# The end of the dilated-attention stage: output weights and seven of eight result rows split during the last segment, and most of the output projection issued ahead of the last merges

## The reference

```python
def dilated_attention_mixer(h, w_in, w_out, rel_bias):
    proj = h @ w_in                       # q, k, v of three groups, and the gate z
    for g, (window, dilation) in enumerate(DILATED_GROUPS):
        o, l = dilated_group_attention(q[g], k[g], v[g], rel_bias, window, dilation)
    wts = jax.nn.softmax(jnp.stack(lses), axis=0)
    o = jnp.sum(wts[..., None] * jnp.stack(outs), axis=0)
    return (o * jax.nn.silu(z)) @ w_out   # the "result" times the output weights
...
h = rms_norm(x, attn_pre_norm)
h = dilated_attention_mixer(h, attn_w_in, attn_w_out, rel_bias)
x = x + rms_norm(h, attn_post_norm)
```

## Time and profile before

| what | us |
|---|---|
| median of 3 runs | 3506.31 (3500.53 to 3507.26) |
| profiled execution, its own time | 3508.67 |
| its span | 3506.3 |
| TensorE matmul busy in the span | 3275.6 (93%) |
| VectorE, ScalarE, GpSimd busy | 1488.2, 1132.5, 1091.1 |
| mean granted TensorE clock | 0.973 of full |

### The profile page before, as it was taken

How to read it: one execution, slowest core, us unless ns; L and a number is a source line. 1 busy time by engine, 2 the same in 40 slices (tenths; PEclk the granted TensorE clock), 3 DMA queues, 4 the chain that set the end, 5 groups by cost and what they waited for, 6 DMA issues and landing times. The chain is left out here.

```text
span 3506.3 us, 49089 instructions
## 1 busy us (share of the span) xinstructions
PE 3275.6 (93%) x19726; PEld 2611.5 (74%) x19726; DVE 1488.2 (42%) x3290; ACT 1132.5 (32%) x2453; POOL 1091.1 (31%) x541
## 2 busy tenths in 40 slices
PE   5999999999999985999899899999999999999997
PEld 4777777878777764778777777777787777777775
DVE  3243132221312225569223345454445734465554
ACT  4333434323333332421312322144342412244421
POOL 1356666322323224233333222211114132212241
PEclk9999999999999997999999999999999999999998
DMA  5313223353423312322524200111003320111113
GB/s 135 72 37 88 70 65 85 86 146 88 121 86 84 101 56 73 111 73 93 206 100 132 82 25 25 31 30 29 25 25 96 113 59 25 31 36 36 31 46 123
DMA packets 324517, 261.00 MB, mean 74 GB/s; under 512 B 75269, under 2 KB 288537, under 8 KB 324298
## 3 DMA queue, kind: packets, MB, share of 16 engines
q10 hardware_dynamic: 122156, 143.83, 13.5%
q1 hardware_dynamic: 202142, 114.09, 11.6%
HBM read 220.89 MB, written 48.58 MB: 77 GB/s over the span
## 5 line engine op out<-in xcount | busy, mean ns | idle before, releaser
L2435 POOL TENSOR_TENSOR w_hi<-w_raw,one 128x1024 fp32r<-128x1024 f32 x170 | 330.4, 1944 | 2078.8 <-PE psum L1411 1016.0
L2587 PE MATMUL psum<-act_hi,w_hi 128*128 128x512 f32 x1280 | 508.9, 398 | 30.5 <-ACT arena L1146 19.2
L1411 PE MATMUL psum<-act_hi,w_hi 128*128 128x512 f32 (+1 forms) x1376 | 511.9, 372 | 21.1 <-DVE arena L1884 13.1
L1411 PE MATMUL psum<-act_lo,w_hi 128*128 128x512 f32 (+1 forms) x1376 | 511.8, 372 | 0.0
L2587 PE MATMUL psum<-act_lo,w_hi 128*128 128x512 f32 x1280 | 509.6, 398 | 0.0
L1411 PE MATMUL psum<-act_hi,w_lo 128*128 128x512 f32 (+1 forms) x1376 | 509.4, 370 | 0.0
L2587 PE MATMUL psum<-act_hi,w_lo 128*128 128x512 f32 x1280 | 505.6, 395 | 0.0
L2438 POOL TENSOR_TENSOR w_lo<-w_raw,w_hi 128x1024 fp32r<-128x1024 f32 x170 | 432.5, 2544 | 13.3
L3333 DVE CUSTOM_DVE_ANT_0 arena<-psum,arena 128x128 f32<-128x128 f32 (+1 forms) x384 | 112.0, 348 | 521.2 <-PE psum L2626 335.4
L1411 PEld LDWEIGHTS psum<-act_hi,w_hi 128*128 128x128 f32 x1376 | 261.8, 190 | 71.8 <-DVE arena L1884 15.1
L2587 PEld LDWEIGHTS psum<-act_hi,w_hi 128*128 128x128 f32 x1280 | 242.7, 190 | 89.7 <-ACT arena L1146 21.3
(11 more groups left out here) (361 smaller groups left out, 5379.4 us busy)
## 6 DMA issues: line engine op xcount, KB each, us to landing
w_raw<-in_attn_w_in SPq DMA_DIRECT2D x80, 512.0 KB, 3.8
w_raw<-in_w_in SPq DMA_DIRECT2D x64, 512.0 KB, 4.0
spare<-in_w_mod ACTq DMA_DIRECT2D x24, 1024.0 KB, 7.8
x<-arena ACTq DMA_DIRECT2D x24, 512.0 KB, 2.9
arena<-x ACTq DMA_DIRECT2D x24, 512.0 KB, 4.4
arena<-in_x ACTq DMA_DIRECT2D x16, 512.0 KB, 5.3
arena<-weight_rows ACTq DMA_DIRECT2D x16, 512.0 KB, 6.4
w_raw<-in_ssm_w_in SPq DMA_DIRECT2D x16, 512.0 KB, 3.9
```

The lines of the kernel that those rows point to most:

```text
L1411: ins = nc.tensor.matmul(psum[:, n % 2, 0:c], w[:, slot % 2, k * P:(k + 1) * P], a[:, k, c0:c0 + c], start=(m == 0), stop=(m == 23))
L2435: G.tensor_tensor(w_hi[:, par], w_raw[:, par], one[:, 0:1].to_broadcast([P, 1024]), ALU.mult).then_inc(slot_hi, 1)
L2587: ins = nc.tensor.matmul(psum[:, h % 2, :], w[:, (3 + j) % 2, k * P:(k + 1) * P], a[:, k, c:c + 512], start=(m == 0), stop=(m == 23))
```

## The change

The rows of `Y1` are split one at a time from inside the last segment, the residents go where the arena is free earlier (`RES_A`: q, k, v of group 1, then rows 0 to 5 of `Y1` once these are split), the gain, x and result tiles of this projection go to other places (`A_ROWS`; the later user of the same functions keeps the old ones as `F_ROWS`), and TensorE issues rows 0 to 6 of the projection for the tiles 0 to 3, tile by tile, as soon as the last segment's own instructions are through. Its `stage_end` becomes a `stage_mark`, which doesn't wait. Row 7 follows for the four tiles. Tiles 4 to 7 are as before but for the residents' addresses.

```diff
-        def y_act(act, base, src, order8, cols=S):
-            for k in range(KT):
...
+        def y_act(act, k):
+            nc.scalar.copy(by_block(act_hi[:, k, 0:S]), by8(Y1[:, k])).then_inc(y_hi, 1)
...
+        def y_dve(dve, k):
+            dve.wait_ge(y_hi, k + 1)
+            nc.vector.tensor_tensor(by_block(act_lo[:, k, 0:S]), by8(Y1[:, k]),
+                                    by_block(act_hi[:, k, 0:S]).bitcast(F32), ALU.subtract).then_inc(y_lo, 1)
...
+        RES_A = resident("res_a", 11264, 13312, 15360, 0, 2048, 4096)
+        A_ROWS = (region(8192, 1024), [region(9216, 1024), region(10240, 1024)],
+                  [region(17408, 1024), region(18432, 1024), region(19456, 1024), region(7168, 1024)])
+        F_ROWS = (F_GAIN, [F_X[:, t] for t in range(2)], [F_T[:, t] for t in range(4)])
...
             def tile(t, last=False):
                 pe.wait_ge(f_scaled, t - 3 if t < 6 else t - 1)
-                res_tile(pe, RES_F, t, 2 * (t % 2), last)
+                res_tile(pe, RES_A, t, 2 * (t % 2), last)
+
+            def rows_but_last(t):
+                for k in range(KT - 1):
+                    if t == 0:
+                        pe.wait_ge(y_lo, k + 1)
+                        pe.wait_ge(slot_split, SLOT_F1 + k + 3)
+                    res_mul(pe, RES_A, k, k, t, 2 * t, used=(k >= 2 and t == 3))
...
-            res_first(pe, SLOT_F1, RES_F, 0)
+            rows_but_last(0)
+            pe.wait_ge(u_logits, 2 * U_DONE)
+            rows_but_last(1)
+            pe.wait_ge(u_pt, U_DONE)
+            rows_but_last(2)
+            pe.wait_ge(u_evac, U_DONE)
+            rows_but_last(3)
+            pe.wait_ge(y_lo, KT)
+            pe.wait_ge(slot_split, SLOT_F1 + KT - 1 + 3)
+            for t in range(4):
+                res_mul(pe, RES_A, KT - 1, KT - 1, t, 2 * t, used=(t == 3)).then_inc(r_mul, 1)
             tile(4)
...
-                pool.wait_ge(stage_done, 3 * stage)
+                if stage > 2:
+                    pool.wait_ge(stage_done, 3 * stage)
+                else:
+                    pool.wait_ge(u_out, NU * (HP - 1) + 2 * NT)
+                    pool.wait_ge(c_freeg, HP - 1)
                 for k in range(2, KT):
                     n = slot0 + k
                     hi, lo = res[k - 2]
+                    if stage == 2 and k >= 5:
+                        pool.wait_ge(y_lo, 2 * (k - 4))
...
-            keep(SLOT_F1, RES_F, 2)
+            keep(SLOT_F1, RES_A, 2)
...
             outputs(HP - 1, NQ - 1)
-            stage_end(pe, 2)
+            stage_mark(pe)
             first_pe(pe)
...
                         k_spread(i)
+                    if hp == HP - 1 and si == 2 and i < KT - 1:
+                        y_act(act, i)
...
             stage_end(act, 2)
-            y_act(act, 0, Y1, True)
+            y_act(act, KT - 1)
...
                     if si == 1 and i == 4:
                         gate(hp, 1)
+                    if hp == HP - 1 and si == 2 and i > 0:
+                        y_dve(dve, i - 1)
...
             stage_end(dve, 2)
-            y_dve(dve, 0, Y1, True)
+            y_dve(dve, KT - 1)
```

More of the change, by code:

```diff
@@ L468, in rest_dve, with f_first @@
                                     act_hi[:, :, c0:c0 + P].bitcast(F32), ALU.subtract).then_inc(t_lo, 1)
-        def f_first(act, xrows, gain):
-            act.dma_start(F_GAIN, spread_rows(gain)).then_inc(f_const, 16)
+        def f_first(act, own, xrows, gain):
+            f_gain, f_x, _ = own
+            act.dma_start(f_gain, spread_rows(gain)).then_inc(f_const, 16)
             for t in range(2):
-                act.dma_start(F_X[:, t], xrows(t)).then_inc(f_loaded[t], 16)
+                act.dma_start(f_x[t], xrows(t)).then_inc(f_loaded[t], 16)
         def f_square_act(act, m, r):
@@ L485, in f_square_act, with f_store_act, f_norm_dve @@
                                  bias=rms_eps[:, 0:1]).then_inc(f_root, 1)
-        def f_store_act(act, m, xrows, orows):
+        def f_store_act(act, own, m, xrows, orows):
             t = m % NT
+            _, f_x, f_t = own
             act.wait_ge(f_sum, m + 1)
-            act.dma_start(orows(t), F_T[:, t % 4]).then_inc(f_stored[t % 2], 16)
+            act.dma_start(orows(t), f_t[t % 4]).then_inc(f_stored[t % 2], 16)
             if t + 2 < NT:
-                act.dma_start(F_X[:, t % 2], xrows(t + 2)).then_inc(f_loaded[t % 2], 16)
-        def f_norm_dve(dve, m, const_n):
+                act.dma_start(f_x[t % 2], xrows(t + 2)).then_inc(f_loaded[t % 2], 16)
+        def f_norm_dve(dve, own, m, const_n):
             t = m % NT
+            f_gain, f_x, f_t = own
             if t == 0:
@@ L504, in f_norm_dve @@
                 dve.wait_ge(f_stored[t % 2], 16 * (m // 2))
-            nc.vector.scalar_tensor_tensor(F_T[:, t % 4], pair_of(t), F_ST[:, t % 4, 2:3], F_GAIN,
+            nc.vector.scalar_tensor_tensor(f_t[t % 4], pair_of(t), F_ST[:, t % 4, 2:3], f_gain,
                                            ALU.mult, ALU.mult).then_inc(f_scaled, 1)
@@ L508, in f_norm_dve @@
             dve.wait_ge(f_loaded[t % 2], 16 * (m // 2 + 1))
-            nc.vector.tensor_tensor(F_T[:, t % 4], F_T[:, t % 4], F_X[:, t % 2], ALU.add).then_inc(f_sum, 1)
+            nc.vector.tensor_tensor(f_t[t % 4], f_t[t % 4], f_x[t % 2], ALU.add).then_inc(f_sum, 1)
         def first_pe(pe):
@@ L555, in stats @@
                 n = NT + t
-                f_store_act(act, t, rows8(x_in), rows8(x1))
+                f_store_act(act, A_ROWS, t, rows8(x_in), rows8(x1))
                 if t >= 4:
                     act.wait_ge(t_rstd, n - 3)
-                nc.scalar.activation(N_JUNK, F_T[:, t % 4], ACT.Square, accum_out=N_ST[:, t % 4, 0:1]).then_inc(t_square, 1)
+                nc.scalar.activation(N_JUNK, A_ROWS[2][t % 4], ACT.Square, accum_out=N_ST[:, t % 4, 0:1]).then_inc(t_square, 1)
                 act.wait_ge(t_square, n + 1)
@@ L568, in first_act @@
                           allow_slow_non_contiguous=True).then_inc(const_loaded, 16)
-            f_first(act, rows8(x_in), io["attn_post_norm"][0])
+            f_first(act, A_ROWS, rows8(x_in), io["attn_post_norm"][0])
             act.wait_ge(const_loaded, 16 * 5)
@@ L602, in norm @@
                     dve.wait_ge(t_square, NT + t - 3)
-                f_norm_dve(dve, t, 1)
+                f_norm_dve(dve, A_ROWS, t, 1)
             def scale(t):
@@ L611, in scale @@
                     dve.wait_ge(t_turned, n - 1)
-                nc.vector.tensor_scalar(N_NORM[:, t % 2], F_T[:, t % 4], N_ST[:, t % 4, 2:3], None, ALU.mult).then_inc(t_scaled, 1)
+                nc.vector.tensor_scalar(N_NORM[:, t % 2], A_ROWS[2][t % 4], N_ST[:, t % 4, 2:3], None, ALU.mult).then_inc(t_scaled, 1)
             def take(t):
@@ L697, in store @@
             def store(t):
-                f_store_act(act, NT + t, rows(x1), rows(x2))
+                f_store_act(act, F_ROWS, NT + t, rows(x1), rows(x2))
             def take(q, t):
@@ L703, in last_act @@
             load_gains(act, 0)
-            f_first(act, rows(x1), io["ssm_post_norm"][0])
+            f_first(act, F_ROWS, rows(x1), io["ssm_post_norm"][0])
             for i in range(2):
@@ L739, in norm @@
                     dve.wait_ge(t_turned, T_DONE + t - 3)
-                f_norm_dve(dve, NT + t, 2)
+                f_norm_dve(dve, F_ROWS, NT + t, 2)
             def take(q, t):
```

## The result

| | before | changed |
|---|---|---|
| median of 4 runs, us | 3506.78 (3500.53 to 3507.53) | 3470.99 (3467.97 to 3477.62) |
| profiled execution, span, us | 3506.3 | 3469.0 |
| mean granted clock | 0.973 | 0.973 |

The ratio is 0.9903, 95% interval 0.9888 to 0.9918: 1.0% less time. The forecast was 3473 us in a range of 3467 to 3485.

What follows compares the result with a forecast made beforehand. TensorE was taken to bound the block of 192 matmuls, idle 35 us before it. Overlapping 168 with the merges puts tile 4 33.5 us earlier: 3508.67 - 33 = 3475.7, median 2.4 lower, 3473; range 3467 to 3485.

Steps and rivals of the forecast that it cites:

- (1): Block before tile 4: TensorE and the split of row 7 tie; gain from 30 to 36 us; chance 0.62.
- Case (4): Tile 0: TensorE stands for residents or splits; gain 20 us if resident 6 came only at 1345; chance 0.03.
- TensorE's part: 168 matmuls, 39.2 us, move right behind the last segment; 24 matmuls, 5.6 us, stay behind the split of row 7.
- The segment: Last segment: TensorE's end slips by 0.9 us and by 0.4 of ScalarE, to 1322.3, between 1321.3 and 1325.
- ScalarE's gaps: Last segment: idle 4.77, 6.06 and 3.69 us; two roundings take 4.1, so the third gap lacks 0.4.
- The merge chain: VectorE behind the last segment: merges late by 8 us; 4 if every split takes 2.0, 11 if every one takes 3.9.
- price "3.9": VectorE's splits in the last segment: one costs 3.9 us where GpSimd works, 2.0 where it idles.
- Rival (2): Row 7: the split chain is clearly last; gain 26 us, or 22 with a further step lost; chance 0.22.
- the tie at row 7: Start of row 7: `act_lo` complete at 1362.0, TensorE there at 1363.0, so TensorE a little later.
- What comes behind: From row 7 on: tile 4 at 1369.3, 33.5 us before 1402.85, then the order unchanged.
- The remark that the gain's load would land just when wanted: First normalisation: load issued at about 1362.5, landing 4.9 us later at 1367.4, 1.3 us before tile 4.
- Case (5): New block: TensorE's clock stays at 1.2 GHz throughout, making it 9 us slower; chance 0.03.

Runs made afterwards that it cites:

- the residents put back: Changed kernel, but GpSimd waits for the end of the stage before splitting weight rows 2 to 7: 3525.9 us against 3510.1 for the kernel before.
- the splits alone: Changed kernel with early splits and residents, but TensorE waiting and ordered as before the change: 3506.9 us against 3510.1 for the kernel before.
- two tiles: Changed kernel with only tiles 0 and 1 issued ahead of the stage's end, tiles 2 and 3 waiting: 3488.7 us against 3510.1 before.
- five repetitions: Changed kernel with VectorE repeating the split of row 7 five times ahead of the one that counts: 3483.8 us against 3510.1 before.
- splits 5 and 6 late: Changed kernel with the splits of rows 5 and 6 moved behind VectorE's last evacuation: 3471.6 us against 3513.6 for the kernel before.
- second profile of the changed kernel: Profile of the same changed kernel, nothing edited, measured again: 3475.4 us against 3512.5 for the kernel before.

## Why the prediction was right

**Cause.** The forecast case was (1): TensorE's 168 matmuls fill the idle block. The three kernels that undo one part each show it: without TensorE's order 34.4 of 35.4 us are lost, with half of it 15.8, and without the early residents all of it and 12.8 more. Case (4), in which tile 0 stands for a resident, is real as a mechanism (the residents put back) but not here.

**TensorE's part.** It was put at 39.2 us for the 168 and 1.5 for the clock, without an idle time. Measured: 1322.81 to 1362.90, which is 40.1, so the clock cost 0.9.

**The segment.** A slip of 1.4 us was worked out, 0.4 measured (34.3 us from the copy of v to the first output matmul against 33.9 to the end of the last instruction before). ScalarE's gaps held their roundings as summed.

**The merge chain.** This is the term that was mis-sized: it was put 8 us late and was 3.4 (last merge at 66.05 us after the copy of v against 62.69). Its price "3.9" for each split beside GpSimd was the part that failed. It comes from two streams without gaps, in which each operation waits for the other engine's, so both are slow. In the segment only the engine that starts second pays. Split 2 began at 1309.20 and took 2.04; GpSimd's operation, which takes 2.35 alone, began 0.03 us behind it and took 4.18. In this profile mainly split 0 (2.94) and one of splits 5 and 6 (5.59 for both) paid.

```profile
1309.23 4.18 POOL L2579 TENSOR_TENSOR res_a_lo<-w_raw,res_a_hi 128x1024 fp32r<-128x1024 f32 x1
```

Part of this was luck. In the run with the splits alone the same two operations came the other way round: GpSimd's began at 1310.14 and took 2.36, and the split, 0.01 us behind it, took a little more than the 3.9 that the prediction had put:

```profile
1310.15 4.15 DVE L354 TENSOR_TENSOR act_lo<-arena,act_hi 128x1024 fp32r<-128x1024 f32 x1 [2.06 <-ACT act_hi L349]
```

So it was in the runs with two tiles (4.14), with five repetitions (4.05) and with splits 5 and 6 late (4.03). In the first three of these four and in the second profile of the changed kernel the last merge was 4.4 to 5.1 us late instead of 3.4. Eight was too much in all of them. Rival (2) was given too much, and the tie at row 7 was a slack of 1.6 to 3.6 us. It changed nothing in the total, since TensorE was last.

The Trainium skill, "SBUF — State Buffer", section "Who interferes with whom", has this as a rule: a VectorE instruction with two SBUF inputs and a GpSimd instruction that reads SBUF exclude each other, and the later one is held until the first ends. The traces agree, for large operations (4.18, 2.94, 4.15) and for the one of 64x32 (2.32).

**What comes behind.** Tile 4 was put 33.5 us earlier and stands 35.4 earlier in D. One microsecond is the slip that didn't come, 0.6 the clock, and 0.3 lies between row 7 and tile 4 (6.0 us where 6.3 was put, half a microsecond of it for the gain's load). The remark that the gain's load would land just when wanted was right in kind: one more split of row 7 was enough for a load to be last, though by the trace it was the gain of the next layer's norm (`in_ssm_pre_norm`, first in the queue), not that of this one. The prediction had no term for this wait, which stands ahead of the first square.

**Slower.** The clock was low for some 2 us at the start of the block (0.55 from 1323 to 1325) and 1.00 from then on; in the second profile of the changed kernel the whole block ran at 1.00 and the 168 matmuls took 39.2 us. Case (5) didn't occur in any profile: the longest low stretch of dense matmuls was 6 us.

## What to carry to other kernels

An engine that is busy 93% of the time may still have one block in which it waits for the last of eight inputs; issue what depends on the other seven first, and then see that each wait in that stream (weights, operands, banks) is met, as one late resident turns the gain into a loss. Work taken off an engine that was hidden is worth nothing by itself, but it can be what lets the bound engine start. Before small operations on a latency chain are moved, look what GpSimd and the load queue start in the same microseconds.

## What the runs showed of the hardware

- A 64x32 operation on VectorE took 2.32 us instead of 0.18 when it met a 128x1024 operation of GpSimd that had begun 0.12 us earlier; a second run had 2.00 in the same way.
- Of two 128x1024 operations of VectorE and GpSimd that began 0.01 to 0.03 us apart the first took its usual 2.0 or 2.4 us and the second 4.2.
- After 35 us without work TensorE's clock stayed at 1.2 GHz for about 4 us of dense matmuls, after 33 us for 5.5 (the splits alone), after 13 us for 6 (two tiles), so the length of the standstill didn't set it. With idle times of 1.4 to 3.1 us between bursts it stayed there for all of 24 us:

```profile
1357.00:1381.00 24.00, 12.82 (x27) 8.36 (x28) 3.98 (x2) 0.00 (x0) 22.00 (x10) 0.50 0.51 155
```

- The load behind the statistics' stores (four of 4 KB) was issued 4.15 and 4.28 us after them, not 2.60, in the two runs in which 512 KB of weights had been issued within half a microsecond ahead of them on another queue. The load itself took its 2.0 us as before.
